# Hyena mixer: spectra folded on VectorE, back transform from half the frequencies, two chains of channel halves

## The reference, cut to what matters

```
p  = xn @ w_in + b_in                       # 256 x 3072
p  = conv_b + sum(pp[:, j:j+L] * conv_w[j] for j in range(3))
x1, x2, v = split(p, 3)
kf = rfft(hyena_filters(...))               # filters of 2L = 512 taps
z  = v
for o, gate in enumerate((x1, x2)):
    z = gate * (irfft(rfft(z, n=2*L) * kf[:, o], n=2*L)[:L] + fbias[o] * z)
return z @ w_out + b_out
```

## Time and profile before

| | us |
|---|---|
| median of three runs | 2899.77 |
| profiled execution | 2904.63 |
| its span, first to last instruction | 2902.8 |
| mean granted TensorE clock | 0.996 of 2.4 GHz |
| TensorE busy | 2854.7 (98%) |
| VectorE busy | 2094.6 (72%) |
| ScalarE busy | 1686.4 (58%) |
| GpSimd busy | 432.1 (15%) |

### The profile page before, as it was taken

How to read it: one execution, slowest core, us unless ns; L and a number is a source line. 1 busy time by engine, 2 the same in 40 slices (tenths; PEclk the granted TensorE clock), 3 DMA queues, 4 the chain that set the end, 5 groups by cost and what they waited for, 6 DMA issues and landing times.

```text
span 2902.8 us, 41709 instructions
## 1 busy us (share of the span) xinstructions
PE 2854.7 (98%) x17504; PEld 2519.1 (87%) x17504; DVE 2094.6 (72%) x1937; ACT 1686.4 (58%) x1713; POOL 432.1 (15%) x279
## 2 busy tenths in 40 slices
PE   8999999999999999999999999999999999999999
PEld 8999988999988888888888796888898888796888
DVE  6787676678768888888888685665666576675664
ACT  6446554545657767767767562554855465362552
POOL 1130331113010000000000002231023133002230
PEclk9999999999999999999999999999999999999999
DMA  7444555544449989889989741455455656540553
GB/s 240 158 133 160 183 183 187 189 146 146 160 158 370 352 342 373 347 342 376 348 334 380 249 131 44 147 190 193 153 160 185 197 159 194 196 146 29 160 185 120
DMA packets 359711, 612.93 MB, mean 211 GB/s; under 512 B 11519, under 2 KB 323925, under 8 KB 324576
## 3 DMA queue, kind: packets, MB, share of 16 engines
q1 hardware_dynamic: 355936, 597.99, 59.1%
q10 hardware_dynamic: 3104, 12.10, 1.2%
q0 software_dynamic: 480, 0.12, 0.0%
HBM read 608.99 MB, written 1.05 MB: 210 GB/s over the span
## 4 chain that ended last, share of the span: by engine, by line
PE 96%; DVE 2%; ACT 1%; DMA 1%; issue 0%; POOL 0%; ACTq 0%; SPq 0%; DVEq 0%; POOLq 0%
PE ps L370 21%; PE ps L371 11%; PE ps L357 8%; PE ps L359 8%; PE ps L358 8%; PE ps L1363 5%; PE ps L1365 5%; PE ps L1364 5%; PE ps L1341 3%; PE ps L1339 3%; PE ps L1340 3%; PE ps L1904 2%; PE ps L739 2%; PE ps L1919 2%; PE ps L1413 1%; PE ps L1872 1%
## 5 line engine op out<-in xcount | busy, mean ns | idle before, releaser
L284 DVE TENSOR_TENSOR wlo<-raw,whi 128x2048 fp32r<-128x2048 f32 (+2 forms) x574 | 1326.1, 2316 | 317.9 <-ACT whi L273 299.2
L273 ACT ACTIVATE whi<-raw 128x2048 fp32r<-128x2048 f32 (+2 forms) x574 | 1085.4, 1893 | 244.6 <-PE ps L371 113.5
L370 PE MATMUL ps<-HXB,whi 128*128 128x512 f32 x1760 | 619.2, 397 | 2.7 <-DVE HXB L498 2.7
L357 PE MATMUL ps<-HX,whi 128*128 128x256 f32 x1808 | 521.1, 288 | 17.1 <-DVE wlo L284 12.3
L358 PE MATMUL ps<-HX,whi 128*128 128x256 f32 x1808 | 512.2, 283 | 0.0
L359 PE MATMUL ps<-HX,wlo 128*128 128x256 f32 x1808 | 512.2, 283 | 0.0
L371 PE MATMUL ps<-HXB,wlo 128*128 128x256 f32 x1760 | 490.9, 279 | 0.0
L370 PEld LDWEIGHTS ps<-HXB,whi 128*128 128x128 f32 x1760 | 330.3, 188 | 83.8 <-DVE HXB L498 3.9
L357 PEld LDWEIGHTS ps<-HX,whi 128*128 128x128 f32 x1808 | 347.5, 192 | 23.4 <-ACT HX L574 10.6
L358 PEld LDWEIGHTS ps<-HX,whi 128*128 128x128 f32 x1808 | 347.7, 192 | 3.4 <-issue 3.3
L359 PEld LDWEIGHTS ps<-HX,wlo 128*128 128x128 f32 x1808 | 347.5, 192 | 0.0
(11 more groups left out here) (338 smaller groups left out, 3978.1 us busy)
## 6 DMA issues: line engine op xcount, KB each, us to landing
raw<-in_c_experts SPq DMA_DIRECT2D x264, 1024.0 KB, 4.8
raw<-in_w_in SPq DMA_DIRECT2D x71, 1024.0 KB, 5.1
raw<-in_ff_w_gate SPq DMA_DIRECT2D x44, 1024.0 KB, 5.4
raw<-in_ff_w_up SPq DMA_DIRECT2D x44, 1024.0 KB, 5.3
raw<-in_ff_w_down SPq DMA_DIRECT2D x32, 1024.0 KB, 4.9
raw<-in_dense_w SPq DMA_DIRECT2D x30, 1024.0 KB, 5.3
raw<-in_hy_w_in SPq DMA_DIRECT2D x24, 1024.0 KB, 5.0
raw<-in_ff_w_down SPq DMA_DIRECT2D x16, 768.0 KB, 4.2
```

Of the source, the lines that this page charges most:

```text
L273: e.activation(m.whi[:, i % NSPLIT, 0:n], m.raw[:, i % NRAW, 0:n], ACT.Copy).then_inc(*k.up("act", "hi", i))
L284: e.tensor_tensor(m.wlo[:, i % NRAW, 0:n], m.raw[:, i % NRAW, 0:n], hi, ALU.subtract).then_inc(*k.up("dve", "lo", i))
L357: e.matmul(o, wh, xh, start=first and t == k0, stop=False)
L370: e.matmul(o[:, :], wh, x[:, :, kx + t, :], start=first and t == k0, stop=False)
```

## The change

In each Hyena mixer:

- The frequencies of group 1 stand in the order that mirrors group 0. The spectra of the two groups are folded first: for even tokens real parts add and imaginary parts subtract, for odd tokens the other way round. `dve_fold` does this in four operations of 128 x 512 per half and convolution. The back transform then sums over 128 frequencies, for even and odd tokens apart: per block again four calls, of 128 columns each.
- The result lies in PSUM with even tokens first, then odd ones; `dve_back` reads it with a stride of 128 elements, in the order of tokens.
- The DFT table loses its back half: 1536 columns for 2048.
- The transposes of half 0 for the first convolution come before the last input panel on TensorE, and their copies and biases on ScalarE before its work for that panel. For that, the turned z of the first convolution lies in another buffer.
- The halves run as two chains: TensorE's, VectorE's and ScalarE's programs interleave them.
- The first two panels of the output projection are taken together: all four column groups over channel blocks 0 to 3, then over 4 to 7.
- The high and low parts of z are made for two blocks at a time.
- GpSimd's instructions are the same, with one more semaphore event.

The core of the diff:

```
 def pe_back(e, k, m, s, o_, c):
-    e.wait_ge(*k.at("Y part", s, o_, 2 * c + 1, 1))
-    for c2 in (2 * c, 2 * c + 1):
-        o = pe_take(e, k, m, "zi", s, o_, c2)
+    re, im, even = spectrum_rows(m, o_, c)
+    odd = re[1], im[1]
+    e.wait_ge(*k.at("odd", s, o_, c))
+    for c2 in range(2):
+        o = pe_take(e, k, m, "zi", s, o_, 2 * c + c2)
         for i in range(2):
-            for n4 in range(4):
-                fr, part = divmod(n4, 2)
-                mm = e.matmul(o[:, i * L:(i + 1) * L], Y[part][...],
-                              dft[:, 2 + part, fr, :], start=n4 == 0, stop=n4 == 3)
+            ch = slice((2 * c2 + i) * 128, (2 * c2 + i) * 128 + 128)
+            for h, rows in enumerate((even, odd)):
+                to = slice(i * L + 128 * h, i * L + 128 * h + 128)
+                e.matmul(o[:, to], rows[0][:, ch], dft[:, 0, 128 * h:128 * h + 128], start=True, stop=False)
+                mm = e.matmul(o[:, to], rows[1][:, ch], dft[:, 1, 128 * h:128 * h + 128], start=False, stop=True)
...
+def pe_out_by_halves(e, k, m, s, x, fresh):
+    taken = []
+    for j in range(2):
+        i = pe_panel(e, k, m)
+        w = weights(m, i, 8, 256)
+        o = pe_take_pair(e, k, m, "g", s, "out", j)
+        for c in range(2):
+            pe_weights_still(e, k, o[c][:, 0:L], w, 128 * c, x, 0, 4, 0, final=False, fresh=None if j or c else fresh)
+        taken.append((i, w, o))
+    for j, (i, w, o) in enumerate(taken):
+        for c in range(2):
+            mm = pe_weights_still(e, k, o[c][:, 0:L], w, 128 * c, x, 4, 8, 0, first=False, fresh=None if j or c else fresh)
+        mm.then_inc(*k.up("mm", "g", s, "out", j))
+        k.note("mm", "used", i)
...
 def pe_hyena(e, k, m, s, last):
...
-    pe_turn_z(e, k, m, s, 0, 0)
+        if j == 10:
+            pe_turn_z(e, k, m, s, 0, 0)
+    pe_forward(e, k, m, s, 0, 0)
     pe_turn_z(e, k, m, s, 0, 1)
-    pe_forward(e, k, m, s, 0, 0)
     pe_forward(e, k, m, s, 0, 1)
     pe_back(e, k, m, s, 0, 0)
+    pe_turn_z(e, k, m, s, 1, 0)
     pe_back(e, k, m, s, 0, 1)
-    pe_turn_z(e, k, m, s, 1, 0)
     pe_forward(e, k, m, s, 1, 0)
...
-    pe_gemm(e, k, m, s, "out", m.HX, range(4), fresh=("zx", s))
+    pe_out_by_halves(e, k, m, s, m.HX, ("zx", s))
+    pe_gemm(e, k, m, s, "out", m.HX, range(2, 4))
...
+def dve_fold(e, k, m, s, o_, c):
+    re, im, even = spectrum_rows(m, o_, c)
+    e.wait_ge(*k.at("Y part", s, o_, 2 * c + 1, 0))
+    e.tensor_tensor(even[0], re[0], re[1], ALU.add).then_inc(*k.up("dve"))
+    e.tensor_tensor(re[1], re[0], re[1], ALU.subtract).then_inc(*k.up("dve"))
+    e.wait_ge(*k.at("Y part", s, o_, 2 * c + 1, 1))
+    e.tensor_tensor(even[1], im[0], im[1], ALU.subtract).then_inc(*k.up("dve"))
+    e.tensor_tensor(im[1], im[0], im[1], ALU.add).then_inc(*k.up("dve", "odd", s, o_, c))
...
 def dve_back(e, k, m, s, o_, c):
...
-            e.scalar_tensor_tensor(z[:, ch, :], o[:, i * L:(i + 1) * L], rn[:, ch:ch + 1], z[:, ch, :], ALU.mult, ALU.add)...
+            zc = z[:, ch, :].rearrange("p (n h) -> p n h", h=2)
+            oc = o[:, i * L:(i + 1) * L].rearrange("p (h n) -> p n h", h=2)
+            e.scalar_tensor_tensor(zc, oc, rn[:, ch:ch + 1], zc, ALU.mult, ALU.add)...
...
     for o_ in range(2):
-        dve_spectrum(e, k, m, s, o_, 0)
-        dve_spectrum(e, k, m, s, o_, 1)
+        dve_spectrum(e, k, m, s, o_, 0, 0)
+        dve_spectrum(e, k, m, s, o_, 0, 1)
+        dve_spectrum(e, k, m, s, o_, 1, 0)
+        dve_fold(e, k, m, s, o_, 0)
+        dve_spectrum(e, k, m, s, o_, 1, 1)
         dve_back(e, k, m, s, o_, 0)
+        dve_fold(e, k, m, s, o_, 1)
+        if o_:
+            dve_low_z(e, k, m, s, 0)
         dve_back(e, k, m, s, o_, 1)
```

More of the change, by code:

```diff
@@ L1810, in pads, with dft_there, dft_back, turned_z @@
     return [rows[:, c % PADS, :] for c in range(24)]
-def dft_view(m):
-    return m.buf(3).rearrange("p (m k n) -> p m k n", m=4, k=2)
+def dft_there(m):
+    return m.buf(3)[:, 0:1024].rearrange("p (m k n) -> p m k n", m=2, k=2)
+def dft_back(m):
+    return m.buf(3)[:, 1024:1536].rearrange("p (m n) -> p m n", m=2)
+def turned_z(m, o_, c):
+    return m.buf(0 if o_ else 10)[:, 1024 * c:1024 * c + 1024]
+def spectrum_rows(m, o_, c):
+    yi = m.buf(2) if o_ else m.HXP[:, BUF:2 * BUF]
+    rows = [y[:, fr * 1024 + c * 512:fr * 1024 + c * 512 + 512] for y in (m.buf(9), yi) for fr in range(2)]
+    both = (m.buf(1) if o_ else m.HXP[:, 0:BUF])[:, 1024 * c:1024 * c + 1024]
+    return rows[0:2], rows[2:4], (both[:, 0:512], both[:, 512:1024])
 def filter_rows(m, f):
@@ L1866, in pe_spectrum @@
     part, c = PIECES[n]
-    dft, src = dft_view(m), m.buf((ODD if part else EVEN)[o_])
+    dft, src = dft_there(m), m.buf((ODD if part else EVEN)[o_])
     e.wait_ge(*k.at("dft", s))
@@ L1886, in pe_turn_z @@
     if o_ == 0:
-        e.wait_ge(*k.at("cv", s, 20 + 3 * c))
+        e.wait_ge(*k.at("cv", s, 19 + 4 * c))
     else:
@@ L1897, in pe_forward @@
 def pe_forward(e, k, m, s, o_, c):
-    dft = dft_view(m)
+    dft, z = dft_there(m), turned_z(m, o_, c)
     e.wait_ge(*k.at("free", "zt", s, o_, 1, c))
@@ L1903, in pe_forward @@
             for j in range(2):
-                mm = e.matmul(o[:, :], dft[:, part, j, fr * 128:fr * 128 + 128],
-                              m.buf(0)[:, j * 1024 + c * 512:j * 1024 + c * 512 + 512], start=j == 0, stop=j == 1)
+                mm = e.matmul(o[:, :], dft[:, part, j, fr * 128:fr * 128 + 128], z[:, 512 * j:512 * j + 512], start=j == 0, stop=j == 1)
             mm.then_inc(*k.up("mm", "zf", s, o_, fr, c, part))
 def pe_back(e, k, m, s, o_, c):
-    dft = dft_view(m)
-    Y = (m.buf(9), m.buf(10))
@@ L1912, in pe_back @@
[L1912 to L1921 removed]
+    dft = dft_back(m)
@@ new lines, in out_rows @@
+def out_rows(k, m, s, j):
+    b = k.bank_of.get(("g", s, "out", j), 0)
+    step = 512 if j < 2 else L
+    return [m.banks[:, 512 * b + step * i:512 * b + step * i + L] for i in range(2)]
+def pe_out_by_halves(e, k, m, s, x, fresh):
[12 more added lines that the diff above has]
+        k.note("mm", "used", i)
@@ L2082, in dve_norm_alone @@
         low_part(e, k, m, s, c - 1, h, "dve")
[L2085 to L2104, removed]
@@ L2112, in dve_back, with products, dve_low_z @@
+def products(m, n):
+    x = m.buf(11)[:, 1024 * (n % 2):1024 * (n % 2) + 1024]
+    return x[:, 0:512], x[:, 512:1024]
+def dve_low_z(e, k, m, s, c):
+    for c2 in (2 * c, 2 * c + 1):
+        t = slice(2 * c2, 2 * c2 + 2)
+        e.wait_ge(*k.at("zh", s, c2))
+        dve_low(e, k, m, m.HX[:, 1, t, :], m.buf8(6)[:, t, :], m.HX[:, 0, t, :], "zx", s, 2 * c2)
+        k.note("dve", "zx", s, 2 * c2 + 1)
 def dve_back(e, k, m, s, o_, c):
@@ L2914, in constants @@
     turned = np.concatenate([np.arange(128), np.arange(255, 127, -1)])
-    m = np.stack([fc[places][:, turned], fs[places][:, turned], fc.T[turned] / 256, fs.T[turned] / 256])
-    c["c_dft"] = np.ascontiguousarray(m.reshape(4, 2, 128, 256).transpose(2, 0, 1, 3).astype(f))
+    there = [w[places][128 * j:128 * j + 128][:, turned] for w in (fc, fs) for j in range(2)]
+    back = [w.T[0:128][:, places] / 256 for w in (fc, fs)]
+    c["c_dft"] = np.ascontiguousarray(np.stack(there + back).transpose(1, 0, 2).astype(f))
     pos = np.linspace(0.0, 1.0, L, dtype=f)[:, None]
```

72 lines of the change are left out of this document (44 added, 28 removed).

## The result

The changed kernel takes 2897.71 us (median of 20 runs, 2891.85 to 2903.17), the kernel before 2901.74 us (20 runs on the same chip, 2897.87 to 2908.21). The ratio is 0.9983, its 95% interval 0.9976 to 0.9990: 4.9 us less, with 2.9 to 7.0 possible. The forecast was 9.4 us less. The side is right, the size about half of what was forecast.

A forecast was written before the change was run, and what follows sets the result against it. TensorE (98% busy) bounds the kernel; in the changed stretch TensorE and VectorE become nearly equal and alternate. Per layer 7.1 us less 2.4 of slow clock gives 4.7, 9.4 for two: 2890.4 us against the median 2899.77, range 2880 to 2898.

The forecast's parts named there:

- Back transform: TensorE's back matmuls in the Hyena mixers: a half takes 3.6 us instead of 6.9, saving 13.2 us per layer.
- Fold: Added VectorE operations before the back matmuls: 2.4 us per half, 9.6 per layer, one GpSimd turn between the first two.
- Early transposes: Half 0's transposes, copies and biases before the last input panel: cost nothing, remove a 2.6 us wait and 1.5 us slow clock.
- The laid-out schedule: Pieces from last input panel to output projection laid in sequence: output starts at 66.6, not 73.7, 7.1 us less per layer.
- Output by halves: Output projection's first 48 matmuls need only half 0, so it starts at 66.6 without the former 2.1 us wait.
- Strided read free: VectorE's scale-and-bias reading PSUM from two places 128 elements apart stays at 0.41 to 0.45 us, nothing lost.
- The rivals of twice and three times the time: Strided PSUM read dearer: up to twice gives 2896 us, chance 0.11; three times or more gives 2903.6 us, chance 0.04.
- the one on the slower side: Kernel slower than before because the strided PSUM read costs three times or more: 2903.6 us at three times, chance 0.04.
- Clock after: Slow TensorE clock behind the new waits: 2.4 us per layer, 4.7 us wait surely, one more about half the time.
- The forecast's own upper bound of 4.5 us: Most slow clock behind the new TensorE waits: two or three periods of 1.5 us, some 4.5 us.
- TensorE the bound, 2859 us: Rival: the fold hides wholly behind TensorE, output starts 20.4 us earlier per layer, 2859 us; chance 0.05.
- The range's high end: Slowest time of the stated range: strided PSUM read at twice the time with more slow clock, 2898 us.

The follow-up runs named there:

- the waits filled: Changed kernel with dummy 128x128 matmuls on TensorE ahead of each wait for a fold; 2887.85 us, ratio 0.9959 to the kernel before.
- the kernel with the folds first: Changed kernel with each fold right behind its own half's products and both back halves before the next transposes; 2874.17 us, ratio 0.9906 to the kernel before.
- the one with the output whole: Changed kernel with the output projection again computed column group by column group over all eight channel blocks; 2896.76 us, ratio 0.9994 to the kernel before.

## Why the prediction was right, and where its size was off

- *Back transform, 3.6 us per half:* right, 0.11 us per instruction at full clock, and on the path, as doubling it showed (a layer 13.3 us longer for back halves that took 13.7 more).
- *Fold, 2.4 us per half, with one turn of GpSimd between its first two operations:* right in pace, order and price.
- *Early transposes, nothing lost, the wait and the slow clock of before gone:* right. Undone, they cost 5.9 and 3.8 us (6.4 for both by the ratios). The 2.6 us wait of before was one for VectorE's last tap; the undone version waits for ScalarE's copies.
- *The laid-out schedule, output at 66.6:* right. Back halves started at 24.6, 34.1, 55.7 and 64.0 (laid out 24.8, 33.0, 54.7, 63.0), and with the waits filled the output came at 66.3.
- *Output by halves:* starts at once, as said; worth 1.6 us per layer.
- *Strided read free:* right, 476 against 479 ns. The rivals of twice and three times the time are out, and with them the one on the slower side. The Trainium skill (PSUM — Partial Sum Buffer, Specifications) states its rule on non-contiguous patterns for matmuls; for VectorE's read at this stride the measurement shows no cost.
- *Clock after, 2.4 us per layer:* this is the term that was mis-sized. I took the 4.7 us wait to trip it once for 1.5 us and one more wait half the time. It went to 0.50 in both layers behind the first 2.1 us wait, 1.6 us lost, and behind the last wait of 4.4 us, where it also lasted longer: 11 of 16 pairs at the lower clock, 2.3 us lost. Starts laid out and seen: at the second back half it had cost 1.1 us (some hides under VectorE), at the last 1.0, at the output 3.3 and 3.4. The forecast's own upper bound of 4.5 us held it. What failed is the price of a period, 1.5 us taken over from the forward matmuls, and the half chance for a second one.
- *TensorE the bound, 2859 us:* out for this order. The rival rested on the fold being hidden. The changed order doesn't hide it; the kernel with the folds first does, mostly: its 59.1 us against 53.3 in that rival.

What remains: with 3.3 and 3.4 us of clock the layers of the two profiled executions are 7.0 us shorter together, against a forecast of 9.4; the ratio shows 4.9 (the two medians as they stand differ by 4.0). The other 2.1 us are inside the interval, which reaches to 7.0. I can't place them. In six kernels of the table, this one among them, the gain by the ratio is 0.6 to 2.8 us smaller than that of the two layers in the one profiled execution, so the changed kernel is no special case.

Nor can a span serve, because code that is the same in all kernels does not take the same time in all executions. Up to the end of the first layer's L1 sums the changed kernel's execution took 2.4 us more than that before, and between the two layers 3.1 us more (796.8 and 793.7; other kernels 793.0 to 796.5). That is why its span is only 1.5 us below that of before. One source of this shows in the matmuls of a feed-forward layer between the two Hyena mixers, first before, then changed (columns of the earlier trace rows):

```profile
2350.00:2500.00 150.00, 150.00 (x867) 131.18 (x866) 95.87 (x79) 75.23 (x73) 42.34 (x25) 1.00 0.65 203
2349.00:2499.00 150.00, 150.00 (x851) 130.03 (x850) 93.85 (x78) 74.80 (x73) 41.84 (x25) 1.00 0.62 198
```

867 matmuls in 150 us are 173 ns each, 851 are 176 ns, both at a granted clock of 1.00. Over a whole feed-forward layer this is some 3 us. Behind the second Hyena layer, which one feed-forward layer follows, three kernels (before and changed among them) take 213.8 us to the end and eight take 210.4 or 210.5. In another feed-forward layer the kernel before had the slower pace (681 matmuls in 120 us, the changed one 694), so it doesn't look like an effect of the change; what sets the pace no view shows.

Luck had a part in the range. The forecast of 2890.4 us was set against three runs with a median of 2899.77; the twenty gave 2901.74, so 2.0 of the 7.3 us between forecast and result lie in the base. The range's high end was meant for a strided read at twice the time, which did not happen; slow clock, the base and the 2.1 us that stay open brought the result there. One reading of the forecast is wrong and enters no sum: VectorE idled 0.95 us before the second group of products of a half only, and 3.74 before a first one.

What I did not see before, though the pieces of my own laying out give it: that with the same pieces in another order the output could start at 58.8. The forecast judged the order given and called the two engines "nearly equal", which reads as if little were left. Some 22 us per run were left, in the order of a few lines.

## What to carry to other kernels

When work is shifted from the engine that bounds to one that feeds it, the feeding engine's order decides what it costs: with the fold behind the other half's products a layer took 69.9 us, with it ahead of them 59.1, as short as without any fold (59.1, one slow period included). Put what the waited-for engine needs next ahead of everything that nobody is waiting for yet, and lay the pieces out in more than the given order before judging a change. Idle gaps on TensorE can be charged twice, once as time and once as a slow clock behind them: here the first 2.1 us wait of each layer cost 1.6 us more that way and the 4.4 us wait 2.3 more. Counting every gap's clock at the forecast's worst (4.5 us per layer) would have come out at 5.2 us in all, near the 4.9 of the ratio, but by luck: the layers lost 3.3 and 3.4, since some of the 1.6 was hidden under VectorE's work.

## What the runs showed of the hardware

- The clock behind a wait. In the stretches looked at, behind each of the 16 waits of 4.1 us or more (seven kernels) the granted clock went to 0.50 for part of what follows (mean over the next 2.8 us 0.50 to 0.69). Behind waits of 1.1 to 2.2 us it did in some and not in others: of the 2.1 us waits before the first back half, both in the changed kernel, neither in the one with the output whole, which has the same order there; in that one it fell behind the next wait, of 2.0 us. So for short waits the clock is a matter of the single execution here, and a profile shows one draw of it.
- Dummy matmuls in such waits pay only where the clock would have fallen: 7 us for the changed kernel, nothing for the one with the folds first.
- The same stream of feed-forward matmuls ran at 173 ns each in one execution and at 176 in another, both at a granted clock of 1.00 (867 and 851 in 150 us). A difference of a few us between two single executions says nothing of a change.
- VectorE reads PSUM in two streams 128 elements apart as fast as in one (476 and 479 ns for 256 columns).
